# Final sums of a decoder layer: half of the columns summed on TensorE with diagonal weight matrices

## The reference, cut to what matters

```python
    combine = jnp.sum(jax.nn.one_hot(e_idx, N_EXPERTS, dtype=jnp.float32)
                      * (g_p[..., None] * top_p)[..., None], axis=-2).astype(h.dtype)
    act = jax.nn.silu(gate) * up * combine[..., None]
    return jnp.einsum('btef,efd->btd', act, w_down)
    ...
    x = x + hier_moe(rms_norm(x, norm2_g), w_group, w_router, w_gate, w_up, w_down)
    ...
    y_prompt = rms_norm(xp, final_g)
    y_sample = rms_norm(xs, final_g)
```

## Time and profile before

| what | value |
|---|---|
| median of 3 runs | 735.75 us (734.45, 735.75, 740.75) |
| time of the profiled execution | 738.03 us |
| its span, first to last instruction | 736.1 us |
| mean granted TensorE clock | 0.947 |
| busy, PE / DVE / ACT / POOL | 86% / 48% / 27% / 18% of the span |

### The profile page before, as it was taken

One profiled execution on the slowest core, in us unless ns is written; L12 is line 12 of the kernel. 1 busy time (PEld: TensorE's weight loads), 2 busy tenths in 40 slices (PEclk: granted clock), 3 DMA queues, 4 the chain that ended last, 5 costly groups with the idle time before them and its releaser, 6 DMA issues.

```text
span 736.1 us, 12734 instructions
## 1 busy us (share of the span) xinstructions
PE 635.4 (86%) x4642; PEld 460.1 (62%) x4643; DVE 357.0 (48%) x689; ACT 198.8 (27%) x403; POOL 129.7 (18%) x229
## 2 busy tenths in 40 slices
PE   5998999999799989997999988978868998888830
PEld 5998999899689879873455654444334554454310
DVE  4657777789986677537554641111111121112138
ACT  6463366433323251251111201111111111111113
POOL 0010010200710010040011255212122223132110
PEclk9999999999989999998999999999998999899975
DMA  9233232323280000017911156999999999969745
GB/s 274 67 84 82 69 87 80 87 58 71 75 296 1 2 0 2 1 60 267 358 48 52 53 186 243 411 411 406 416 417 412 395 392 399 376 223 415 308 151 217
DMA packets 73591, 146.34 MB, mean 199 GB/s; under 512 B 14804, under 2 KB 50984, under 8 KB 65343
## 3 DMA queue, kind: packets, MB, share of 16 engines
q1 hardware_dynamic: 67967, 137.02, 50.5%
q0 software_dynamic: 5568, 8.54, 3.3%
HBM read 138.77 MB, written 16.07 MB: 210 GB/s over the span
## 4 chain that ended last, share of the span: by engine, by line
PE 64%; DMA 16%; DVE 10%; issue 4%; ACT 2%; POOL 1%; SPq 1%; POOLq 1%; DVEq 0%; ACTq 0%
PE ps L1824 20%; PE ps L2154 13%; DMA wd<-w_down 11%; PE ps L2070 8%; PE ps L1919 8%; DMA xg<-h_rows,gcur 2%; DVE XX L1519 2%; PE ps L2168 1%; DVE x L1743 1%; PE ps L2186 1%; PE ps L1837 1%; PE ps L2092 1%; PE ps L1773 1%; DMA expert_rows<-yo,osid 1%; PE ps L1913 1%
## 5 line engine op out<-in xcount | busy, mean ns | idle before, releaser
L2154 PE MATMUL ps<-gu,xT 128*64 128x256 f32 x1024 | 133.5, 405 | 27.9 <-DMA wd<-w_down 21.3
L2154 PEld LDWEIGHTS ps<-gu,xT 128*64 128x64 f32 x1024 | 74.2, 144 | 82.7 <-issue 34.3
L1824 PE MATMUL ps<-hhi,whi 128*128 128x256 f32 (+1 forms) x416 | 121.0, 291 | 3.4 <-DVE wlo L1219 1.8
L1824 PE MATMUL ps<-hlo,whi 128*128 128x256 f32 (+1 forms) x416 | 118.7, 285 | 0.0
L1824 PE MATMUL ps<-hhi,wlo 128*128 128x256 f32 (+1 forms) x416 | 118.6, 285 | 0.0
L1692 DVE SCALAR_TENSOR_TENSOR gact<-gth,ps 128x128 f32<-128x128 f32 x32 | 9.2, 288 | 156.0 <-ACT gth L967 156.0
L1824 PEld LDWEIGHTS ps<-hhi,whi 128*128 128x128 f32 x416 | 79.7, 192 | 7.9 <-issue 4.8
L1824 PEld LDWEIGHTS ps<-hhi,wlo 128*128 128x128 f32 x416 | 80.0, 192 | 0.0
L1824 PEld LDWEIGHTS ps<-hlo,whi 128*128 128x128 f32 x416 | 79.7, 192 | 0.0
L2154 PE MATMUL ps<-wd,aT 128*64 128x512 f32 x256 | 64.7, 628 | 0.4 <-ACT aT L971 0.4
L2070 PE MATMUL ps<-wout,yT 128*128 128x512 f32 x128 | 57.7, 599 | 0.0
(11 more groups left out here) (387 smaller groups left out, 942.9 us busy)
## 6 DMA issues: line engine op xcount, KB each, us to landing
gu<-w_gate SPq DMA_DIRECT2D x32, 1024.0 KB, 9.0
gu<-w_up SPq DMA_DIRECT2D x32, 1024.0 KB, 11.2
wd<-w_down SPq DMA_DIRECT2D x32, 1024.0 KB, 14.7
wraw<-w_in SPq DMA_DIRECT2D x26, 512.0 KB, 3.8
wout<-w_out SPq DMA_DIRECT2D x1, 4096.0 KB
yk<-expert_rows SPq DMA_DIRECT2D x8, 512.0 KB, 6.4
x<-x_prompt SPq DMA_DIRECT2D x4, 512.0 KB, 6.5
s<-state_delta SPq DMA_DIRECT2D x4, 512.0 KB, 6.1
```

The costliest lines, as they stand in the source:

```text
L1824: last = mm(ps[:, 2 * (n % 2) + half, 0:hi - lo], weights[:, c, :], h[:, c, lo:hi], start=c == 0 and j == 0, stop=c == KT - 1 and j == len ...
L2154: last = mm(ps[g * CAP:(g + 1) * CAP, bank, 0:width], left(c), right(c, g), start=c == 0, stop=c == steps - 1)
```

## The change

The final sums are split by columns. The left half (columns 0 to 511) stays on VectorE. The right half (columns 512 to 1023) is summed on TensorE into PSUM bank i for tile i: x times the identity, plus each of the two expert rows times a diagonal matrix that holds its weights.

- VectorE, after the last expert, first makes ten diagonal matrices `dw[i][k]` (identity times weight). Then `add_rows` covers the left half alone, and `finish` multiplies the two halves in two instructions, the right one read from PSUM.
- TensorE waits for the first diagonal matrix, issues the five identity matmuls, then eight matmuls of constants into bank 7, then waits for all ten diagonal matrices, and then for each tile for its loads, and issues the two diagonal matmuls.
- ScalarE squares the right half from PSUM, then the left half from `x`, adds the two sums (Identity with the other sum as bias), and takes the square root.
- SyncE writes a tile out when both its halves are finished.
- A semaphore (`rep_ready`) is given up; its one use counts on `g_ready` (to 5) instead, in an earlier stage.

```diff
+        weigh = Region(K1 + 24576, K2)
+        dw = [[weigh(f"dw{i}{k}", [P, P]) for k in range(2)] for i in range(NT)]
+        LEFT, RIGHT = slice(0, D // 2), slice(D // 2, D)
...
-                sp.wait_ge(fin_ready, i + 1)
+                sp.wait_ge(fin_ready, 2 * i + 2)
...
-                act.wait_ge(fin_added, 2 * i + 2)
+                right, both_halves = ns[0:n, 12, i:i + 1], ns[0:n, 13, i:i + 1]
                 if i:
-                    act.wait_ge(x1_squared, 2 * (NT + i))
-                copy(fsq[0:n, :], x[0:n, ORDER[i], :], ACT.Square, accum_out=ss[0:n, i:i + 1]).then_inc(x1_squared, 1)
-                act.wait_ge(x1_squared, 2 * (NT + i) + 1)
-                copy(ss[0:n, i:i + 1], ss[0:n, i:i + 1], ACT.Sqrt, scale=1.0 / D, bias=epsc[0:n, :]).then_inc(x1_squared, 1)
+                    act.wait_ge(x1_squared, 2 * NT + 4 * i)
+                act.wait_ge(fin_summed, i + 1)
+                copy(fsq[0:n, RIGHT], ps[0:n, i, :], ACT.Square, accum_out=right).then_inc(x1_squared, 1)
+                act.wait_ge(fin_added, 2 * NT + 2 * i + 2)
+                copy(fsq[0:n, LEFT], x[0:n, ORDER[i], LEFT], ACT.Square, accum_out=ss[0:n, i:i + 1]).then_inc(x1_squared, 1)
+                act.wait_ge(x1_squared, 2 * NT + 4 * i + 2)
+                copy(both_halves, ss[0:n, i:i + 1], ACT.Identity, bias=right).then_inc(x1_squared, 1)
+                act.wait_ge(x1_squared, 2 * NT + 4 * i + 3)
+                copy(ss[0:n, i:i + 1], both_halves, ACT.Sqrt, scale=1.0 / D, bias=epsc[0:n, :]).then_inc(x1_squared, 1)
...
+            vec.wait_ge(down_done, NE)
+            for i in range(NT):
+                n = rows(i)
+                for k in range(2):
+                    ts(dw[i][k][0:n, 0:n], ident[0:n, 0:n], wgt[0:n, k, i:i + 1], None, ALU.mult).then_inc(fin_added, 1)
+
...
-                        vec.wait_ge(fin_added, 2 * i + 1)
-                    stt(out=x[0:n, ORDER[i], :], in0=yk[i][0:n, k, :], scalar=wgt[0:n, k, i:i + 1], in1=x[0:n, ORDER[i], :], op0=ALU.mult,
-                        op1=ALU.add).then_inc(fin_added, 1)
+                        vec.wait_ge(fin_added, 2 * NT + 2 * i + 1)
+                    stt(out=x[0:n, ORDER[i], LEFT], in0=yk[i][0:n, k, LEFT], scalar=wgt[0:n, k, i:i + 1], in1=x[0:n, ORDER[i], LEFT],
+                        op0=ALU.mult, op1=ALU.add).then_inc(fin_added, 1)
...
-                stt(out=x[0:n, ORDER[i], :], in0=x[0:n, ORDER[i], :], scalar=rstd[0:n, i:i + 1], in1=gfb[0:n, :], op0=ALU.mult,
-                    op1=ALU.mult).then_inc(fin_ready, 1)
+                for half, sums in ((LEFT, x[0:n, ORDER[i], LEFT]), (RIGHT, ps[0:n, i, :])):
+                    stt(out=x[0:n, ORDER[i], half], in0=sums, scalar=rstd[0:n, i:i + 1], in1=gfb[0:n, half], op0=ALU.mult,
+                        op1=ALU.mult).then_inc(fin_ready, 1)
...
+            pe.wait_ge(fin_added, 1)
+            for i in range(NT):
+                n = rows(i)
+                mm(ps[0:n, i, :], ident[0:n, 0:n], x[0:n, ORDER[i], RIGHT], start=True, stop=False)
+            for _ in range(8):
+                mm(ps[:, 7, :], ones, cst[:, C_ID:C_ID + 512], start=True, stop=True)
+            pe.wait_ge(fin_added, 2 * NT)
+            for i in range(NT):
+                n = rows(i)
+                pe.wait_ge(x_in[i], 3 * 16)
+                for k in range(2):
+                    last = mm(ps[0:n, i, :], dw[i][k][0:n, 0:n], yk[i][0:n, k, RIGHT], start=False, stop=k == 1)
+                last.then_inc(fin_summed, 1)
```

More of the change, by code:

```diff
@@ L382, in pair @@
             return [sem(f"{name}{z}") for z in range(2)]
-        rep_ready, spread, eG_ready, D_ready, DT_ready = sem("rep_ready"), sem("spread"), sem("eG_ready"), sem("D_ready"), sem("DT_ready")
+        spread, eG_ready, D_ready, DT_ready = sem("spread"), sem("eG_ready"), sem("D_ready"), sem("DT_ready")
         kb_ready, scored, rows_done, A_ready, rows_scaled = (
@@ L418, in build @@
             sem("more_" + n) for n in ("otok", "osid", "pe", "act", "vec", "out"))
-        fin_added, fin_ready = sem("fin_added"), sem("fin_ready")
+        fin_added, fin_ready, fin_summed = sem("fin_added"), sem("fin_ready"), sem("fin_summed")
         wr_in, cleared = sem("wr_in"), sem("cleared")
@@ L1377, in _ @@
                     link(nc.vector.tensor_copy(rowsr[0:8, :], ps[0:8, 5, :]))
-                    nc.vector.tensor_tensor(rowsr[32:40, :], ps[0:8, 5, :], rowsr[0:8, :], ALU.subtract).then_inc(rep_ready, 1)
+                    nc.vector.tensor_tensor(rowsr[32:40, :], ps[0:8, 5, :], rowsr[0:8, :], ALU.subtract).then_inc(g_ready, 1)
                 if n - 1 in AT_Q:
@@ L1741, in add_rows @@
                     if k:
-                        vec.wait_ge(fin_added, 2 * i + 1)
-                    stt(out=x[0:n, ORDER[i], :], in0=yk[i][0:n, k, :], scalar=wgt[0:n, k, i:i + 1], in1=x[0:n, ORDER[i], :], op0=ALU.mult,
-                        op1=ALU.add).then_inc(fin_added, 1)
+                        vec.wait_ge(fin_added, 2 * NT + 2 * i + 1)
+                    stt(out=x[0:n, ORDER[i], LEFT], in0=yk[i][0:n, k, LEFT], scalar=wgt[0:n, k, i:i + 1], in1=x[0:n, ORDER[i], LEFT],
+                        op0=ALU.mult, op1=ALU.add).then_inc(fin_added, 1)
             def finish(i):
                 n = rows(i)
-                vec.wait_ge(x1_squared, 2 * (NT + i) + 2)
+                vec.wait_ge(x1_squared, 2 * NT + 4 * i + 4)
                 link(nc.vector.reciprocal(rstd[0:n, i:i + 1], ss[0:n, i:i + 1]))
@@ L1925, in _ @@
                 for z, h, B in pairs:
-                    pe.wait_ge(rep_ready, 1)
+                    pe.wait_ge(g_ready, 5)
                     pe.wait_ge(z_evac, NZ)
```

## The result

The change makes the kernel slower: a median of 742.74 us over 22 runs against 735.73 over 22 runs before, 7.0 us more, outside the predicted range and on the other side of the forecast, though within one per cent. The ratio is of fast runs alone, without the five slowest runs after the change, which lie over 1.5 per cent above the fastest: 1.0073 with a 95% interval of 1.005 to 1.0095, that is 5.4 us (3.7 to 7.0).

The account below looks back on a forecast made before the run. VectorE was taken to set the end: 2.7 us gained from finish(0) on, 2.2 lost by its later start behind TensorE's sum, leaving 0.5 off the median: 735.3 us, range 732.0 to 738.5.

Parts of the forecast that it names:

- Sixteen of this form took 7.11 us at the full clock, 0.44 each: TensorE ahead of finish(0): price of one 512-column matmul, 0.44 us at full clock, 0.84 at the lower level.
- the 15 matmuls: TensorE from 708.6: five identities, eight constants and two diagonal ones, giving the sample tile's sum at 716.9.
- TensorE becomes the bound: Rival, chance 0.12: clock stays at 1.2 GHz through all 15 matmuls; VectorE ends 3.8 us later, time 739.6.
- the signs of being wrong: In the tail: VectorE not waiting before finish(0), a period above 3.3 us, or the end moving over 4 us.
- The clock: TensorE's granted clock after its pause: lower level for 3.5 us from 708.6, then full clock.
- the other case that the rows had shown: TensorE's restart after a 4.50 us pause: clock back 6.1 us on; here that would mean a loss of 0.7.
- VectorE's part: VectorE in the last stage: period 3.04 us instead of 3.98, and 12.3 from finish(0) to its end.
- the 65 ns for PSUM: VectorE's right halves: extra cost per PSUM read by the skill; the forecast counted none, with it gain 0.2.
- from the sum to the root: ScalarE on the first tile: squares, Identity, table load and root, 3.4 us after TensorE's sum.
- The table rival: Rival, chance 0.03: Identity needs its own table, so ScalarE loads twice a tile; end 8.9 later, 744.7.
- The ten matrices: New VectorE work after the last expert: 3.1 us, done near 709.9 under the wait for loads, costed at nothing.
- Early TensorE: Rival, chance 0.10: TensorE starts by 707.0 and VectorE alone sets the end; gain 3.8 us, time 732.0.

Follow-up runs that it names:

- the second profile: The changed kernel profiled again, unaltered: tail 33.3 us, finish(0) 21.0 us behind the last expert; one run, no ratio.
- The run with the sample tile on VectorE: Changed kernel without constants, root's table loaded early, sample tile summed and finished on VectorE and ScalarE as before the change: 0.9971 of the kernel before.
- the run with the matrices late: Sample tile on VectorE, no constants, root's table loaded early, diagonal matrices made after GpSimd's last scatter: 0.9958 of the kernel before the change.
- the run with three identities and the table early: Changed kernel without constants, three identity matmuls ahead of the sample tile's diagonal ones, root's table loaded before the first square: 0.9973 of the kernel before.

## Why the prediction was wrong

**The step that failed: "Sixteen of this form took 7.11 us at the full clock, 0.44 each".** The sixteen were records, and they are eight matmuls. Line 2123 has 26 records in the trace before, while the code asks `keep_going` for 3, 2 and 8 matmuls, 13 in all:

```profile
L2123 PE MATMUL ps<-cst x26: 592/592/676, 420.6 to 433.8; 128*128 128x512 f32 x26
```

(592 ns is the length of one record; the records overlap, 0.44 us from one to the next.) The same shows in the earlier trace rows: eight records where `down` issues four matmuls. A 512-column fp32 matmul costs 0.86 us at the full clock and about twice that, 1.71, at the lower one, where the weight loads of the first profile begin 0.85 us apart, two to a matmul. The Trainium skill ("FP8 and Floating Point Precision", section "TensorE Precision Notes") says that true fp32 takes four passes through the array; worked out from that, an estimate, 4 x 512 columns at 2.4 GHz are 0.853 us, and the trace agrees with 0.86.

So the 15 matmuls, for which I had 8.3 us with the lower clock in it, took 16.5 (and 15.0 in the second profile). The sample tile's sum came 19.6 us behind the last expert instead of 11.3, `finish(0)` at 22.8 instead of 14.7, and the end 8.1 later than forecast: -0.5 + 8.1 = 7.6, where the profile shows 7.5. Of the 8.2 us that the matmuls took beyond the forecast, some 6.3 are the price: worked out with 0.86 and 1.71 us a matmul and the forecast's 3.5 us at the lower level, the 15 would have taken 14.6. The remaining 1.9 are the clock (0.4 in the second profile). The price is shown three times over: eight matmuls fewer, eight more and half of the columns moved the tail by the part that it gives them.

**The rival that came nearest** is "TensorE becomes the bound", which had 0.12. Its effect and its point of decision held: a loss once the sum ends after 717.4, 11.8 behind the last expert. Its condition did not: the clock did not stay at 1.2 GHz through all 15 matmuls, it came back 6.5 us behind the restart. The loss came from the price, which this rival had at the same wrong 0.44, so that its 3.8 us lie near the measured 5.4 by luck. Of the signs of being wrong that the prediction named, the third showed: the end moved by more than 4 us in the profile.

**The clock**, as a size, was off as well: I took 3.5 us at the lower level. In the first profile it was low from about 702.6 to 709.4, 6.5 us behind the restart, close to the other case that the rows had shown; in the second it fell only 1.4 us after the restart and was back 3.4 later. Windows of the first, then two of the second, whose restart was at 705.82:

```profile
702.00:703.00 1.00, 0.09 (x1) 0.09 (x2) 1.00 (x6) 0.00 (x0) 0.44 (x1) 0.79 0.03 12
703.00:704.00 1.00, 1.00 (x2) 0.01 (x1) 0.52 (x3) 0.00 (x0) 0.00 (x0) 0.50 0.35 119
...
709.00:710.00 1.00, 1.00 (x3) 0.51 (x2) 0.22 (x1) 0.00 (x0) 0.00 (x0) 0.80 0.98 369
```

```profile
707.00:708.00 1.00, 1.00 (x2) 0.40 (x2) 0.00 (x0) 0.00 (x0) 0.00 (x0) 0.59 0.00 0
...
710.00:711.00 1.00, 1.00 (x3) 0.50 (x2) 0.88 (x2) 0.00 (x0) 0.00 (x0) 0.71 0.98 389
```

**What held.** TensorE began 3.05 us behind the last expert, as forecast, behind a branch of 3.83 us:

```profile
L456 PEldq COMPARE_BRANCH  x1: 3828/3828/3828, 699.0 to 699.0; - x1
```

VectorE's part held: the period 3.04, and from `finish(0)` to the end 12.2 us for 12.3. The right halves from PSUM took 0.75, as the left ones did. So the 65 ns for PSUM, an estimate from the cycles that the Trainium skill ("VectorE: DVE Perf Modes", section on the TRN2 errata) gives, are not seen. ScalarE took 3.3 us from the sum to the root for 3.4, the Identity 0.29. The table rival is out: one load, ahead of the first root. The ten matrices took 1.94 us instead of 3.1, under the wait for the loads. Early TensorE, the rival at 3.8 us of gain, did not occur. The run with the sample tile on VectorE reached its state another way, with VectorE alone setting the end, and has 4.0 in the tail.

## What to carry to other kernels

Before a price is taken from a group of records, count them against the instructions that the code issues. Work handed to an idle engine is not free when the first result of a serial chain hangs on it: what matters is the time of the first result, so give the first, smallest tile to the engine that would otherwise wait, and keep filler matmuls out of the queue in front of it. Compare the stage that was changed from one event to another, since spans of single executions can differ by more in stages that were not touched.

## What the runs showed that I had not expected

In three of the eleven profiles in which VectorE makes the diagonal matrices at the time of GpSimd's last scatter, that scatter took 1.70 to 1.90 us; every other scatter of all thirteen profiles, some 36 in each, took 1.04 at most. In the three, the loads were issued 5.6 to 6.3 us behind the last expert instead of 4.1 to 4.4. The other eight are not free of a trace: in each of them one of the diagonal matrices, begun beside the scatter, took 0.42 to 0.51 us, where the longest took 0.31 to 0.32 in the three and 0.29 in the run with the matrices late. So in all eleven one of the two engines lost time, VectorE under 0.25 us or GpSimd 0.7 to 0.9, and where the two did not overlap neither did. The scatter in the profile with twice the constants:

```profile
705.02 1.90 POOL L1153 DMA_INDIRECT expert_rows<-ysb,scur  x1 [1.34 <-DVE ysb L1735]
```

The matrices in the same profile (shortest, median and longest, ns), and below them those of the changed kernel's first profile:

```profile
L1749 DVE TENSOR_SCALAR dw<-cst,wgt x10: 213/268/312, 705.2 to 706.8; 128x128 f32<-128x128 f32 x8, 8x8 f32<-8x8 f32 x2
```

```profile
L1749 DVE TENSOR_SCALAR dw<-cst,wgt x10: 214/268/433, 701.6 to 703.2; 128x128 f32<-128x128 f32 x8, 8x8 f32<-8x8 f32 x2
```

The Trainium skill ("Advanced Engine Details and Errata", section "VectorE Performance Modes") says that VectorE's second port is shared with GpSimd, and that GpSimd's instructions and those of VectorE in a two-port mode block each other. That fits all eleven, but no run shows which mode the matrices' instructions use, nor what decides which engine waits, so the cause stays open. In two of the three TensorE came to the sample tile's rows after they had landed, and the tail is not longer by the slow scatter; the third is the run with three identities and the table early.

The clock's fall varied between executions: the five identity matmuls took 6.35 and 7.81 us in the two profiles of the changed kernel, and 6.30 to 7.89 in the seven profiles that have all five ahead, which moves the end by up to 1.6 us where they stand in the chain.
